# Where the ring of weights, the activations and the gated product begin in on-chip memory: three offsets modulo 2048 bytes in place of one

## The chip, the cores and the metric

The kernel runs on one core of a Trainium2 chip. The metric is the device time of one execution in microseconds. Addresses below are byte addresses within a partition of the on-chip memory (SBUF); each tensor occupies the same byte range in all 128 partitions.

## The reference

Two transformer blocks follow each other on 256 tokens of width 1024, all in float32. What matters here is that nearly all the work is products of activations with large weight matrices:

```
h = rmsnorm(x); proj = h @ w_in            # 1024 x 3072, then three mixers (two attentions, a short convolution)
x = x + group_rmsnorm(y) @ w_out           # 1024 x 1024
x = x + (silu(h @ w_gate) * (h @ w_up)) @ w_down      # 1024 x 2816, twice, and 2816 x 1024
# second block
h = rms_norm(x); proj = h @ w_in_2         # 1024 x 5888, spatial gating and a dilated attention
x = x + (gates[0] * (y_a @ w_branch_a) + gates[1] * (y_b @ w_branch_b)) @ w_out
up = h2 @ w_up; x = x + (gelu(conv(a)) * val) @ w_down; return rms_norm(x)
```

## The kernel before, in words

**Split precision.** Every float32 operand of a large product is split in two float32r tensors, a high part and the rest. A product is then three matmuls: high by high, high by low, low by high. The tensors that hold split activations are hx (the normalised input; hh and hl are its high and low half), yx (the mixer's output, later the second feed-forward's input; yh and yl) and G (the gated product of a feed-forward). Each has for each block of 128 features 256 high values and then 256 low ones, so 2048 bytes for a block.

**The ring.** The weights arrive as a stream of 113 units of 128 x 2048 values, numbered u = 0 to 112. Unit u lives in place u % 3 of a ring. SyncE starts its DMA into raw (line 456) when the unit three earlier has been split; ScalarE casts raw to whi (line 530, the high part) when TensorE is done with the unit three earlier; VectorE subtracts whi from raw into wlo (line 983, the low part); TensorE waits for that (`ready`) and uses the unit. raw, whi and wlo have three places each, 8192 bytes long, all of them allocated in a row, raw first.

**TensorE's instructions.** Each matmul loads its own stationary 128 x 128 tile (an LDWEIGHTS instruction) ahead of it, while the matmul before it streams. There are three kinds of unit:
- Pairs (`tiles`, lines 1606 and 1607): a 128 x 128 tile of whi is stationary and 512 columns stream (256 high, 256 low, adjacent in hx, yx or G); then the same tile of wlo with the 256 high columns alone. A unit has 16 pairs. The feed-forwards' gate and up products, the first down product and the second block's gate projections are of this kind: units 16 to 37 (hx), 38 to 48 (G), 61 to 71 (hx), 80 to 101 (yx).
- Narrow threes (`three`, lines 1599 to 1601): a tile of whi, again of whi and of wlo is stationary, and 256 columns of hx or yx stream. 48 matmuls a unit: units 6, 7, 9, 10, 11 and 76 to 79 (hx), 12 to 15 and 72 to 75 (yx). Unit 8 has the roles exchanged, 256 columns of whi or wlo streaming over tiles of hx.
- Wide threes (the same lines): hx or G is stationary and 512 columns of whi or wlo stream, 24 matmuls a unit: units 0 to 5 and 49 to 60 (hx), 102 to 112 (G).

**Addresses.** The allocator places tensors one after the other and starts each at a multiple of 32 bytes. A fixed region of 16384 bytes and four small constants of 32 bytes each come first, so raw begins at 16512, which is 128 modulo 2048. The nine ring places (8192 bytes each), sq (8192), hx (16384) and x follow. Therefore every place of raw, whi and wlo, and hx, begins at 128 modulo 2048. x has 8224 bytes, so yx after it begins at 160. G and gates share an address, behind a gap of LEAD float32 values, and begin at 128. All tiles that TensorE reads from these tensors lie at multiples of 512 bytes from the tensor's start.

Of the kernel before, what the change touches and what calls it, by code (L numbers as in the profile page):

```python
# [18 lines left out]
F32R = mybir.dt.float32r  # L19
# [5 lines left out]
P = 128  # L25
T = 256
TT = T // P
D = 1024
KT = D // P
# [3 lines left out]
UNIT = 16 * P  # L33
# [3 lines left out]
WARM_UP = 8  # L37
RING = 3

LEAD = 160  # L40

D_SB, D_CH, D_CV = 256, 512, 256
H_SB, H_CH = D_SB // HD, D_CH // HD
# [189 lines left out]
def build(nc, A, out):  # L233
    with ExitStack() as ctx:
        def sb(name, shape, dt=F32, scope=ctx):
            return scope.enter_context(nc.sbuf_tensor(name, shape, dt))
# [2 lines left out]
            return ctx.enter_context(nc.semaphore(name))  # L239

        raw = [sb(f"raw{s}", [P, UNIT]) for s in range(RING)]
        whi = [sb(f"whi{s}", [P, UNIT], F32R) for s in range(RING)]
        wlo = [sb(f"wlo{s}", [P, UNIT], F32R) for s in range(RING)]


        sq = sb("sq", [P, KT, T])
        hx = sb("hx", [P, KT, 2, T], F32R)

        x_gain = sb("x", [P, KT + KT * T])
        attn_gain, x = x_gain[:, 0:KT], x_gain[:, KT:KT + KT * T].rearrange("p (k t) -> p k t", k=KT)  # L250
        yx = sb("yx", [P, KT, 2, T], F32R)
        hh, hl = hx[:, :, 0, :], hx[:, :, 1, :]
        yh, yl = yx[:, :, 0, :], yx[:, :, 1, :]
        side = sb("side", [P, 2, T])
# [30 lines left out]
        sg = ExitStack()  # L285
        sb("before_G", [P, LEAD], scope=sg)
        G = sb("G", [P, FF_K, 2, T], F32R, scope=sg)
# [6 lines left out]
        s2 = ExitStack()  # L294
        sb("before_gates", [P, LEAD], scope=s2)
        gates = sb("gates", [P, 2, KT, T], scope=s2)
# [1940 lines left out]
```

## Time and profile before

| | |
|---|---|
| median of 3 runs | 692.86 us (692.68 to 693.03) |
| the profiled execution | 692.9 us, its span 691.2 us |
| TensorE matmul (PE) | busy 682.4 us, 99% of the span, 4118 instructions |
| weight load (PEld) | busy 601.3 us, 87% |
| VectorE (DVE) | busy 498.5 us, 72% |
| ScalarE (ACT) | busy 401.5 us, 58% |
| granted TensorE clock | 0.998 in the mean |

The span runs from the first to the last instruction; the rest of the time lies around it. The end of a matmul in the profile is modelled, and the modelled durations of adjacent matmuls overlap. So a matmul's cost is read from the distance between starts, not from its duration.

### The profile page before, as it was taken

How to read it: one execution, taken by the hardware profiler on the slowest of the kernel's cores; microseconds unless marked ns; L12 is line 12 of the kernel's file. 1: busy time of each engine (PE TensorE's matmuls, PEld its weight loads, DVE VectorE, ACT ScalarE, POOL GpSimd, SP SyncE). 2: the span in 40 equal slices, each digit the busy share in tenths (PEclk: the TensorE clock that was granted, in tenths of full speed). 3: DMA queues.
4: the chain of work that ended last, by engine and by line, in shares of the span. 5: the costliest groups of instructions: out<-in, count | busy, mean ns of one | idle time of the engine just before them, and what ended most of it. 6: DMA issues, size and time to landing. Idle time of an engine off the chain costs nothing.

```text
span 691.2 us, 10061 instructions
## 1 busy us (share of the span) xinstructions
PE 682.4 (99%) x4118; PEld 601.3 (87%) x4118; DVE 498.5 (72%) x689; ACT 401.5 (58%) x504; POOL 9.3 (1%) x25
## 2 busy tenths in 40 slices
PE   8999999999999999999999999999999999999996
PEld 7889999888888888888878888899988888888885
DVE  6866676979886766766565477687779988887453
ACT  7865865755555544455457565564557666664342
POOL 1000000003000000000000000000000000000000
PEclk9999999999999999999999999999999999999999
DMA  8863225655555555555435346444455555554511
GB/s 326 317 238 129 86 98 184 218 186 183 183 200 187 213 192 183 178 188 187 180 123 181 123 142 224 146 183 160 183 197 199 192 180 187 192 201 176 215 61 61
DMA packets 19773, 124.05 MB, mean 179 GB/s; under 512 B 2320, under 2 KB 3472, under 8 KB 5520
## 3 DMA queue, kind: packets, MB, share of 16 engines
q1 hardware_dynamic: 18432, 120.07, 48.7%
q10 hardware_dynamic: 1296, 3.35, 1.4%
q8 instruction: 32, 0.52, 0.3%
q14 instruction: 13, 0.11, 0.0%
HBM read 122.36 MB, written 1.05 MB: 179 GB/s over the span
## 4 chain that ended last, share of the span: by engine, by line
PE 90%; DVE 4%; ACT 3%; issue 1%; DMA 1%; DVEq 0%; ACTq 0%
PE psum L1606 34%; PE psum L1607 18%; PE psum L1599 10%; PE psum L1601 10%; PE psum L1600 10%; PE psum L1595 2%; DVE wlo L983 2%; ACT whi L530 2%; PE psum L1646 1%; PE psum L1649 1%; PE psum L2078 1%; PE psum L1652 1%; DMA x<-in_xT 1%; PE psum L2126 0%; DVE gates L1501 0%
## 5 line engine op out<-in xcount | busy, mean ns | idle before, releaser
L983 DVE TENSOR_TENSOR wlo<-raw,whi 128x2048 fp32r<-128x2048 f32 x110 | 251.7, 2290 | 76.4 <-ACT whi L530 76.4
L530 ACT CAST whi<-raw 128x2048 fp32r<-128x2048 f32 x110 | 209.6, 1908 | 42.8 <-PE psum L1601 37.7
L1606 PE MATMUL psum<-hx,whi 128*128 128x512 f32 x528 | 184.3, 395 | 0.0
L1607 PE MATMUL psum<-hx,wlo 128*128 128x256 f32 x528 | 146.9, 278 | 0.0
L1606 PE MATMUL psum<-yx,whi 128*128 128x512 f32 x352 | 123.2, 393 | 1.0 <-DVE yx L994 1.0
L1606 PEld LDWEIGHTS psum<-hx,whi 128*128 128x128 f32 x528 | 99.1, 188 | 23.3 <-issue 0.2
L1607 PEld LDWEIGHTS psum<-hx,wlo 128*128 128x128 f32 x528 | 99.4, 188 | 0.0
L1607 PE MATMUL psum<-yx,wlo 128*128 128x256 f32 x352 | 99.3, 282 | 0.0
L1606 PEld LDWEIGHTS psum<-yx,whi 128*128 128x128 f32 x352 | 66.1, 188 | 15.3 <-DVE yx L994 1.6
L1607 PEld LDWEIGHTS psum<-yx,wlo 128*128 128x128 f32 x352 | 66.7, 190 | 0.0
L1606 PE MATMUL psum<-G,whi 128*128 128x512 f32 x176 | 61.1, 394 | 0.0
L1599 PE MATMUL psum<-whi,hx 128*128 128x512 f32 (+1 forms) x144 | 55.9, 388 | 0.0
L1601 PE MATMUL psum<-whi,hx 128*128 128x512 f32 (+1 forms) x144 | 54.5, 378 | 0.0
L1600 PE MATMUL psum<-wlo,hx 128*128 128x512 f32 (+1 forms) x144 | 54.4, 378 | 0.0
L1607 PE MATMUL psum<-G,wlo 128*128 128x256 f32 x176 | 48.8, 277 | 0.0
L1599 PE MATMUL psum<-hx,whi 128*128 128x256 f32 x144 | 41.5, 288 | 0.1
L1601 PE MATMUL psum<-hx,wlo 128*128 128x256 f32 x144 | 40.8, 283 | 0.0
L1600 PE MATMUL psum<-hx,whi 128*128 128x256 f32 x144 | 40.8, 283 | 0.0
L1606 PEld LDWEIGHTS psum<-G,whi 128*128 128x128 f32 x176 | 33.0, 188 | 7.7
L812 ACT COPY us<-psum 128x512 f32<-128x512 f32 x22 | 12.9, 585 | 42.4 <-PE psum L1607 42.4
L805 ACT COPY side<-psum 128x512 f32<-128x512 f32 x22 | 12.8, 584 | 40.0 <-PE psum L1607 40.0
L1599 PE MATMUL psum<-yx,whi 128*128 128x256 f32 x128 | 36.0, 282 | 0.0
(271 smaller groups left out, 1107.7 us busy)
## 6 DMA issues: line engine op xcount, KB each, us to landing
raw<-in_stream SPq DMA_DIRECT2D x110, 1024.0 KB, 4.7
raw<-in_stream SPq DMA_DIRECT2D x8, 256.0 KB, 5.4
relb<-in_relb ACTq DMA_DIRECT2D x1, 1536.0 KB, 7.7
raw<-in_stream SPq DMA_DIRECT2D x2, 512.0 KB, 7.4
x<-in_xT SPq DMA_DIRECT2D x3, 256.0 KB, 5.6
out_t<-sq SPq DMA_DIRECT2D x4, 160.0 KB, 2.4
final_gain<-in_final_gain ACTq DMA_DIRECT2D x1, 512.0 KB, 3.7
bsp<-in_bsp ACTq DMA_DIRECT2D x1, 384.0 KB, 3.3
```

Of the source, the lines that this page charges most:

```text
L530: act.copy(whi[s][:], raw[s][:]).then_inc(unit_hi, 1)
L805: act.copy(side[:], psum[:, 0:2, T:2 * T]).then_inc(gate_side, 1)
L812: act.copy(us[:], psum[:, 2:4, T:2 * T]).then_inc(up_side, 1)
L983: dve.tensor_tensor(wlo[s][:], raw[s][:], whi[s][:], ALU.subtract).then_inc(unit_lo, 1)
L1595: return pe.transpose(out_, in_, ident[:])
L1599: pe.matmul(dst, stat[0], mov[0], start=first, stop=False, **kw)
L1600: pe.matmul(dst, stat[0], mov[1], start=False, stop=False, **kw)
L1601: return pe.matmul(dst, stat[1], mov[0], start=False, stop=last, **kw)
L1606: pe.matmul(bank[b][:], stat[0], mov, start=first, stop=False, skip_group_check=True)
L1607: return pe.matmul(bank[b][:, 0:T], stat[1], mov[:, 0, :], start=False, stop=last, skip_group_check=True)
L1646: pe.matmul(bank[6 + t][:], hh[:, k, c], whi[u][:, w], start=k == 0, stop=False)
L1649: pe.matmul(bank[6 + t][:], hh[:, k, c], wlo[u][:, w], start=False, stop=False)
```

## The change

hx moves in front of whi and wlo; whi and wlo of one place now stand together (whi0, wlo0, then whi1, wlo1, then whi2, wlo2); a gap of 32 bytes is put before the second and before the third place; yx moves between the second place and the second gap. LEAD falls from 160 to 144 values, which is 64 bytes less and takes up the two gaps. No instruction, wait or order changes.

```diff
-LEAD = 160
+LEAD = 144
...
         raw = [sb(f"raw{s}", [P, UNIT]) for s in range(RING)]
-        whi = [sb(f"whi{s}", [P, UNIT], F32R) for s in range(RING)]
-        wlo = [sb(f"wlo{s}", [P, UNIT], F32R) for s in range(RING)]
+        whi, wlo = [None] * RING, [None] * RING
+
+        def place(s):
+            whi[s] = sb(f"whi{s}", [P, UNIT], F32R)
+            wlo[s] = sb(f"wlo{s}", [P, UNIT], F32R)
+
+        hx = sb("hx", [P, KT, 2, T], F32R)
+        place(0)
+        sb("before_second", [P, 8])
+        place(1)
+        yx = sb("yx", [P, KT, 2, T], F32R)
+        sb("before_third", [P, 8])
+        place(2)
         sq = sb("sq", [P, KT, T])
-        hx = sb("hx", [P, KT, 2, T], F32R)
...
-        yx = sb("yx", [P, KT, 2, T], F32R)
```

Start modulo 2048, in bytes:

| tensor | before | after |
|---|---|---|
| raw, all three places | 128 | 128 |
| whi and wlo, place 0 / 1 / 2 | 128 / 128 / 128 | 128 / 160 / 192 |
| hx, G, gates | 128 | 128 |
| yx | 160 | 160 |
| sq, x | 128 | 192 |

What is allocated after x and before G (side, rb, cols, ident, ones and others), and the first block's mixer tensors, shift by 64 bytes. The second block's tensors behind LEAD keep their place.

## Rows read from the trace of the kernel before

**Rows 1.** The page: busy time and granted clock by fortieth.
```profile
PE 682.4 (99%) x4118; PEld 601.3 (87%) x4118; DVE 498.5 (72%) x689; ACT 401.5 (58%) x504; POOL 9.3 (1%) x25
...
PEclk9999999999999999999999999999999999999999
```

**Rows 2.** All waits of TensorE: who waited for whom, total us, times, longest.
```profile
PE psum L1947 <- POOL ones L474: 1.1, 1, 1.1
PE psum L1606 <- DVE yx L994: 1.0, 2, 0.5
PE psum L1646 <- ACT whi L535: 0.7, 1, 0.7
```

**Rows 3.** Groups of matmuls, kinds apart; names are moving,stationary.
```profile
L1606 PE MATMUL psum<-hx,whi 128*128 128x512 f32 x528 | 184.3, 395 | 0.0
L1606 PE MATMUL psum<-yx,whi 128*128 128x512 f32 x352 | 123.2, 393 | 1.0 <-DVE yx L994 1.0
L1606 PE MATMUL psum<-G,whi 128*128 128x512 f32 x176 | 61.1, 394 | 0.0
```

**Rows 4.** Line 1606 in four windows: hx, G, yx, then hx in the gates.
```profile
L1606 PE MATMUL psum<-hx,whi x305: 391/394/396, 138.7 to 244.1; 128*128 128x512 f32 x153
...
L1606 PE MATMUL psum<-G,whi x176: 391/394/396, 244.5 to 305.1; 128*128 128x512 f32 x176
...
L1606 PE MATMUL psum<-yx,whi x113: 389/390/391, 585.5 to 624.3; 128*128 128x512 f32 x113
...
L1606 PE MATMUL psum<-hx,whi x81: 394/398/404, 393.3 to 421.6; 128*128 128x512 f32 x81
```

**Rows 5.** Line 1599, narrow threes with hx, then with yx.
```profile
L1599 PE MATMUL psum<-hx,whi x49: 283/283/284, 481.1 to 498.4; 128*128 128x256 f32 x49
L1599 PEld LDWEIGHTS psum<-hx,whi x48: 191/192/193, 481.4 to 498.3; 128*128 128x128 f32 x48
...
L1599 PEld LDWEIGHTS psum<-yx,whi x64: 186/188/190, 452.9 to 474.9; 128*128 128x128 f32 x64
L1599 PE MATMUL psum<-yx,whi x64: 277/279/282, 453.0 to 475.0; 128*128 128x256 f32 x64
```

**Rows 6.** Line 1599, wide threes with G; line 1595, transposes.
```profile
L1599 PE MATMUL psum<-whi,G x64: 388/389/390, 635.5 to 678.4; 128*128 128x512 f32 x64
...
L1595 PE MATMUL psum<-ident,S x16: 271/273/273, 368.6 to 370.2; 128*128 128x128 f32 x16
```

**Rows 7.** Timeline: a matmul and the weight load for the next start together.
```profile
481.84 0.28 PE L1599 MATMUL psum<-hx,whi 128*128 128x256 f32 x1
481.84 0.19 PEld L1600 LDWEIGHTS psum<-hx,whi 128*128 128x128 f32 x1
481.96 0.28 PE L1600 MATMUL psum<-hx,whi 128*128 128x256 f32 x1
481.96 0.19 PEld L1601 LDWEIGHTS psum<-hx,wlo 128*128 128x128 f32 x1
```

**Rows 8.** The two splits of a unit from 60 to 680 us, and VectorE's wait.
```profile
L530 ACT CAST whi<-raw x103: 1885/1909/1932, 59.8 to 668.4; 128x2048 fp32r<-128x2048 f32 x103
  PE psum L1601: 36.6, 14
...
L983 DVE TENSOR_TENSOR wlo<-raw,whi x103: 2274/2292/2321, 61.7 to 670.4; 128x2048 fp32r<-128x2048 f32 x103
  ACT whi L530: 74.4, 69
```

**Rows 9.** Busy time by engine in one stretch.
```profile
139.10:244.40 105.30, 105.30 (x610) 92.04 (x609) 85.80 (x119) 56.01 (x58) 5.40 (x8) 1.00 0.54 190
```

## The prediction

> **What bounds the kernel now.** I read the page's busy times first: the matmul engine is busy for 682.4 of the span's 691.2 us, at full granted clock in every fortieth [rows 1]. Next its waits: three entries, 2.8 us in all [rows 2]. So the weights are always there in time, and the time is the sum of the distances between matmul starts. The third view is one line's first and last start with its count, which gives that distance. Pairs with hx streaming: 305 starts from 138.7 to 244.1 us, so 105.4/304 = 346.7 ns a pair. With G: 60.6/175 = 346.3. With yx: 38.8/112 = 346.4 [rows 4]. Narrow threes with hx: 48 threes in 17.3 us, 120.1 ns a matmul. With yx: 63 threes in 22.0 us, 116.4 ns [rows 5]. Wide threes: 63 in 42.9 us, 227.0 ns [rows 6].
>
> The reader is to see two things. First, 256 columns more cost 227.0 - 120.1 = 107 ns, so a matmul of 256 columns has about 13 ns that are not streaming, and one of 512 too; a pair has 346.7 - 3 x 107 = 26, again 13 each. These 13 ns are the only thing that a changed address can move. Second, the narrow threes with yx are 3.7 ns shorter than those with hx, with the same shapes and weights. What differs is the address: yx begins at 160 modulo 2048, hx and the weights at 128. Each matmul starts together with the weight load for the next [rows 7], and with hx that load too is recorded longer (192 against 188 ns) [rows 5]. So where the streamed operand begins relative to the loaded one does matter, in that one kind. In the pairs the same 32 bytes make no difference: 346.4 with yx, 346.7 and 346.3 with hx and G, and the readings are good to 1 ns.
>
> **The change part by part.** No instruction is added, removed or moved. I write the offset as streamed minus weights. Today it is 0 with hx and G and +32 with yx. After: with hx and G it is 0, -32, -64 in places 0, 1, 2; with yx +32, 0, -32. Where the weights stream (wide threes) it is 0, +32, +64.
>
> Pairs. There are 1056 [rows 3]. Units by place (u % 3): units 16 to 37 give 7, 8, 7 in places 0, 1, 2; units 38 to 48 give 4, 3, 4; units 61 to 71 give 3, 4, 4; units 80 to 101 (yx) give 7, 7, 8. Places 0, and place 1 of yx, have offsets that the trace shows, and they cost the same (346.3 to 346.7): nothing there. New are -32 in 8+3+4+8 = 23 units, 368 pairs, and -64 in 7+4+4 = 15 units, 240 pairs: 608 pairs. Bounds: the dearest row of a pair is the gates', 28.3/80 = 353.8 ns, 7.1 more [rows 4]; from below, a 128-column load and matmul need 1.6/15 = 107 ns in the transposes [rows 6], which allows a 256-column matmul 13 less and a pair 26 less. Far apart, so I take the nearest rows, which are pairs at 0 and at +32: no change. Ends kept: -15.8 us (608 x 26 ns) and +4.3 us (608 x 7.1 ns).
>
> Narrow threes. hx in place 1 (units 7, 10, 76, 79) and place 2 (11, 77), and unit 8, where the weights stream at +64: 7 x 48 = 336 matmuls leave the offset 0, which costs 120.1. They can fall to 116.4 or stay; I take half of it: -336 x 1.85 ns = -0.62 us, ends -1.24 and 0. yx in place 1 (13, 73): 96 matmuls come to the offset 0, so 3.7 ns each: +0.36. yx in place 2 (14, 74): 96 at -32, half: +0.18, ends 0 and +0.36. The sum is -0.08 us.
>
> Wide threes. Place 1 (units 1, 4, 49, 52, 55, 58, 103, 106, 109, and half of 112) and place 2 (2, 5, 50, 53, 56, 59, 104, 107, 110): 228 + 216 = 444 matmuls at +32 and +64. They are 512-column matmuls as half of the pairs' are, and pairs did not care for +32: nothing. Ends: -3.7 ns each as in the threes, -1.6 us; +3.5 each (half of the gates' 7.1), +1.6.
>
> A rule of the Trainium skill bears on this. The page "TensorE: Matmul & The Clock Gate", in "Step-by-step: what each phase is for", says that TensorE reads SBUF through two independent ports, so that loading the next weights takes nothing from the running matmul. The trace disagrees in one kind, 120.1 against 116.4 ns; by that rule every term here would be nothing and the time that of before.
>
> The engines beside it. ScalarE's casts take 1885 to 1932 ns and VectorE's subtractions 2274 to 2321, while TensorE reads another place all the time [rows 8]. So narrow a spread over 103 units leaves nothing that staggered places could save them. If they changed anyway, VectorE waits 74.4 us for the casts and ScalarE 36.6 for TensorE [rows 8], and that cover holds: a cast 5% longer is 0.1 us against those waits. In the other direction, pairs kept to 391 to 396 ns [rows 4] while VectorE was busy for 85.8 and ScalarE for 56.0 of 105.3 us [rows 9], so their accesses don't slow TensorE. The shift by 64 bytes of x, sq and the first mixer's tensors touches short operations and float32 matmuls; priced at nothing, as all these stay multiples of 32 from where they were; if ten of the short ones on the path grew by 10 ns it would be 0.1 us.
>
> Sum: 0 - 0.08 + 0 = -0.1 us on the profiled execution's 692.9 (span 691.2 and 1.7 around it), so 692.8. The median of the runs is 692.86, the same to 0.1.
>
> **The rivals.**
> (B) The 13 ns shrink wherever the offset isn't 0, as in the threes. For it: 120.1 against 116.4 ns. Against it: the pairs with yx, at +32, have kept their 26. In full, 1216 matmuls of the 608 pairs and 444 wide ones lose 3.7 ns each, -4.5 and -1.6, and the narrow ones -1.24 + 0.36: -7.0 us, 685.9. If only one of the two negative offsets does it, about half: 689.4.
> (C) The other side, slower. The gates show that the same instructions at the same addresses can run in a dearer rhythm: 353.8 ns a pair for more than 28 us, from the small attention matmuls on until other small ones follow, and in nothing else different from the 346.7 [rows 4]. If the load begins 32 or 64 bytes ahead of the streamed operand, it may meet it in the same place of the memory shortly after the start, and the matmuls lock into that rhythm. Place: the pairs at a negative offset. Price: 608 x 7.1 = +4.3, with the yx threes' +0.72 in full: 697.9. With -32 alone (368 pairs, +2.6, and +0.7): 696.2. With -64 alone (240 pairs, +1.7, and +0.4): 695.0. It decides as soon as some 200 pairs are in it, for that is 1.4 us. For it: the rhythm exists. Against it: it appears only in 6 of 66 units, and yx's offset never brought it.
> (D) The placement doesn't do what it says, or is of no consequence, the threes included: 692.9. In the numbers this is my forecast.
>
> **How the numbers follow.** A measurement of this kernel tells about 0.2%, 1.4 us, from no change. My forecast with (D): 0.46. B in full or part: 0.29. C: 0.25. All of the forecast's own spread (-1.24 to +0.72) is within 0.2%: 691.6 to 693.6. B lies below 691.5 and C above 694.3. So faster 0.29, same 0.46, slower 0.25. The range takes in C whole but for its last part and the nearer half of B: 688.0 to 697.2.
>
> **What would show it.** The starts of line 1606 by unit: 346.7 ns a pair in all three places would bear me out; 340 or so in places 1 and 2 of units 16 to 60 shows B; 353 there shows C. Line 1599 in units 77 and 78, next to each other in places 2 and 0, gives the threes' effect within one stage; units 72 to 75 give yx at +32, 0 and -32. L530 and L983 should keep 1909 and 2292 ns. I am wrong if the pairs move by more than 2 ns in either new offset, or if the gates' dear stretch (units 61 to 66) ends or spreads: its end alone is 96 x 7.1 = -0.7 us. A change in the other kernel-wide quantities (granted clock, waits of TensorE over 3 us) would mean that I read the wrong resource.

## The result and the profile after

The changed kernel takes 699.24 us (699.17 to 699.81, four runs) against 692.94: a ratio of 1.0095 with a 95% interval of 1.0083 to 1.0107; the medians lie 6.3 us apart. The prediction was 692.8 with a range up to 697.2. The profiled execution took 699.8 us, its span 698.1, which is 6.9 more than before.

The page after. Work and clock are as they were, and the matmul engine's busy time has grown by the whole difference [rows 1]:
```profile
PE 689.3 (99%) x4118; PEld 602.6 (86%) x4118; DVE 498.6 (71%) x689; ACT 401.1 (57%) x504; POOL 9.4 (1%) x25
...
PEclk9999999999999999999999999999999999999999
```

Line numbers are higher by 10. All waits of TensorE after; 3.0 us where it was 2.8 [rows 2]:
```profile
PE psum L1616 <- DVE yx L1004: 1.2, 3, 0.5
PE psum L1957 <- POOL ones L484: 1.1, 1, 1.1
PE psum L1656 <- ACT whi L545: 0.7, 1, 0.7
```

Line 1616, pairs in the first feed-forward and the down product (they answer to rows 4):
```profile
L1616 PE MATMUL psum<-hx,whi x305: 388/398/403, 139.3 to 246.6; 128*128 128x512 f32 x153
...
L1616 PE MATMUL psum<-G,whi x176: 388/398/403, 247.0 to 308.8; 128*128 128x512 f32 x176
```
A pair costs 107.3/304 = 353.0 ns with hx (346.7 before) and 61.8/175 = 353.1 with G (346.3). The mean over the three places leaves no room for a cheap place. The timeline shows them one by one; these are the first matmuls of units 33, 34, 35 and 36, in places 0, 1, 2, 0, sixteen pairs apart:
```profile
218.71 0.40 PE L1616 MATMUL psum<-hx,whi 128*128 128x512 f32 x1
...
224.37 0.39 PE L1616 MATMUL psum<-hx,whi 128*128 128x512 f32 x1
...
230.03 0.40 PE L1616 MATMUL psum<-hx,whi 128*128 128x512 f32 x1
...
235.66 0.40 PE L1616 MATMUL psum<-hx,whi 128*128 128x512 f32 x1
```
5.66, 5.66 and 5.63 us: 353.8 ns in place 0 (offset 0, as before the change), 353.8 in place 1 (-32), 351.9 in place 2 (-64). **Place 0 is as dear as the others, although its own offset did not change.** (These distances run from unit to unit and take in the step between two units.)

The wide threes (first matmuls of units 103 to 106, places 1, 2, 0, 1; 24 matmuls apart) and the narrow ones with hx (units 77, 78, 79 and what follows; 48 apart):
```profile
636.15 0.40 PE L1609 MATMUL psum<-whi,G 128*128 128x512 f32 x1
...
641.76 0.40 PE L1609 MATMUL psum<-whi,G 128*128 128x512 f32 x1
...
647.26 0.39 PE L1609 MATMUL psum<-whi,G 128*128 128x512 f32 x1
...
652.73 0.40 PE L1609 MATMUL psum<-whi,G 128*128 128x512 f32 x1
```
```profile
486.14 0.28 PE L1609 MATMUL psum<-hx,whi 128*128 128x256 f32 x1
...
491.59 0.28 PE L1609 MATMUL psum<-hx,whi 128*128 128x256 f32 x1
...
497.35 0.28 PE L1609 MATMUL psum<-hx,whi 128*128 128x256 f32 x1
...
503.03 0.40 PE L1616 MATMUL psum<-yx,whi 128*128 128x512 f32 x1
```
Wide: 233.8 ns at +32, 229.2 at +64, 227.9 at 0, where all were 227.0 [rows 6]. Narrow: 113.5 ns at -64, 120.0 at 0, 118.3 at -32, where all were 120.1 [rows 5].

Where the time went, from the starts of the same matmuls in both traces: for each unit the mean distance of undisturbed starts times the number of matmuls, difference after minus before, in us.

| kind | place 0 | place 1 | place 2 | sum |
|---|---|---|---|---|
| pairs with hx, G (units 16 to 71) | +1.36 | +1.26 | +1.18 | +3.8 |
| pairs with yx | +0.07 | +0.63 | +0.63 | +1.3 |
| wide threes | +0.19 | +1.42 | +0.46 | +2.1 |
| narrow threes | +0.04 | +0.02 | -0.55 | -0.5 |

Together +6.7 of the span's +6.9 us. A single entry depends by 0.1 us or so on which starts are counted as undisturbed.

### The profile page after: what moved, and what is told of

Its sections match the earlier page's. It is cut to its first block, busy times and chain, and to the rows that moved or that the text cites. A ratio compares the mean times of both kernels' runs of the same rounds, so it can differ in the third digit from the quotient of the medians.

```text
span 698.1 us, 10061 instructions
## 1 busy us (share of the span) xinstructions
PE 689.3 (99%) x4118; PEld 602.6 (86%) x4118; DVE 498.6 (71%) x689; ACT 401.1 (57%) x504; POOL 9.4 (1%) x25
## 4 chain that ended last, share of the span: by engine, by line
PE 91%; DVE 4%; ACT 3%; issue 1%; DMA 1%; DVEq 0%; ACTq 0%
PE psum L1616 35%; PE psum L1617 18%; PE psum L1609 10%; PE psum L1611 10%; PE psum L1610 10%; PE psum L1605 2%; DVE wlo L993 2%; ACT whi L540 2%; PE psum L1656 1%; PE psum L1659 1%; PE psum L2088 1%; PE psum L1662 1%; DMA x<-in_xT 1%; PE psum L2136 0%; DVE gates L1511 0%
## 5 line engine op out<-in xcount | busy, mean ns | idle before, releaser
L1616 PE MATMUL psum<-hx,whi 128*128 128x512 f32 x528 | 186.9, 398 | 0.0
L1616 PE MATMUL psum<-yx,whi 128*128 128x512 f32 x352 | 124.7, 397 | 1.2 <-DVE yx L1004 1.2
L1616 PEld LDWEIGHTS psum<-yx,whi 128*128 128x128 f32 x352 | 66.1, 188 | 17.3 <-DVE yx L1004 2.1
```

The source lines that it names most:

```text
L1616: pe.matmul(bank[b][:], stat[0], mov, start=first, stop=False, skip_group_check=True)
```

## The experiments

**Theories.** H: the cost of a matmul follows from the offset (streamed minus weights; the expectation of the first run calls this part R), and pairs have besides that two rhythms, about 346.7 and 353.3 ns a pair, one of which is handed on from unit to unit. Rivals: the order and neighbourhood of the tensors or the other engines' writes cost the time (O, E); each unit pays for its own offset alone (L); only the change of offset from unit to unit is dear (M); the rhythm belongs to the addresses and nothing else changes it (N).

In all layouts below LEAD is set so that G and gates stand as said. First four layouts, run together.

**The order alone.** hx first, whi and wlo of a place together, all places at 128:
```diff
         hx = sb("hx", [P, KT, 2, T], F32R)
         place(0)
-        sb("before_second", [P, 8])
         place(1)
-        yx = sb("yx", [P, KT, 2, T], F32R)
-        sb("before_third", [P, 8])
         place(2)
+        sb("gap0", [P, 8])
+        yx = sb("yx", [P, KT, 2, T], F32R)
```


> The changed order of allocation (hx first, whi and wlo of a place together) with all three places at 128 modulo 2048, hx and G at 128, yx at 160: the offsets of before, and the rest of the memory shifted by 32 bytes. Theory R (relative offset, streamed minus weights, is all that counts): 692.9 us, pairs at 346.7 ns in all places, narrow threes 120 with hx and 116.7 with yx. Rival O (the order, or the neighbourhood of raw, whi and wlo, or the shift of the small tensors costs the time): 699 us. Between them if both have a part.

Measured: 693.31 us, ratio 1.0005 (0.9996 to 1.0014). Line 1615, the same stretch as in rows 4, 105.4/304 = 346.7 ns:
```profile
L1615 PE MATMUL psum<-hx,whi x305: 391/391/391, 138.9 to 244.3; 128*128 128x512 f32 x153
```
O is out: the order, with the rest of the memory shifted by 32 bytes, costs nothing that can be measured.

**Place 1 alone at 160**, places 0 and 2 at 128:
```diff
         place(0)
-        sb("before_second", [P, 8])
+        place(2)
+        sb("gap0", [P, 8])
         place(1)
         yx = sb("yx", [P, KT, 2, T], F32R)
-        sb("before_third", [P, 8])
-        place(2)
```


> Place 1 alone at 160; places 0 and 2 at 128; hx, G 128, yx 160. Theory H (rhythm handed on: TensorE's pairs have two rhythms, 346.7 and about 353.5 ns, a unit at offset -32 throws them into the dear one and a later unit at offset 0 stays in it): places 0 and 2 are dear as well, 353.7 ns with hx and G, some 38 units by 16 pairs by 6.8 ns = +4.1 us, place 1 with yx +0.7, wide threes of place 1 (228 by 6.8 ns) +1.6, narrow ones about 0: 699.3 us. Rival L (each unit pays for its own offset alone): only place 1 is dear, 13 units by 16 by 6.7 = +1.4, +0.7, +1.6: 696.6 us, with 346.7 ns in places 0 and 2.

Measured: 698.48 us, ratio 1.0082 (1.0067 to 1.0097). Units 33 to 36 again (places 0, 1, 2, 0):
```profile
218.35 0.40 PE L1615 MATMUL psum<-hx,whi 128*128 128x512 f32 x1
...
224.00 0.39 PE L1615 MATMUL psum<-hx,whi 128*128 128x512 f32 x1
...
229.65 0.39 PE L1615 MATMUL psum<-hx,whi 128*128 128x512 f32 x1
...
235.29 0.40 PE L1615 MATMUL psum<-hx,whi 128*128 128x512 f32 x1
```
5.65, 5.65 and 5.64 us, 353 ns in every place. Place 0 follows place 2, both at offset 0 as before the change, and is dear all the same. So L (696.6) is out; the time is 0.8 us below H's 699.3. Where the dear rhythm begins can be seen too. These are the first matmuls of units 16 and 17 and the last pair of unit 17, fifteen pairs on:
```profile
121.99 0.39 PE L1615 MATMUL psum<-hx,whi 128*128 128x512 f32 x1
...
127.53 0.40 PE L1615 MATMUL psum<-hx,whi 128*128 128x512 f32 x1
...
132.84 0.40 PE L1615 MATMUL psum<-hx,whi 128*128 128x512 f32 x1
```
Unit 16, in place 1 at -32, took 346 ns a pair, and unit 17, in place 2 at offset 0, 354. No other matmul stands between the two, and with all places at 128 unit 17 ran at 346.7. So it was not a dear unit at -32 that handed its rhythm on, as H had it: here the rhythm switched where the offset went from -32 to 0, and the later units kept it.

**All places 32 bytes on, and all 64 bytes on**, constant offsets:
```diff
         hx = sb("hx", [P, KT, 2, T], F32R)
+        sb("gap0", [P, 8])
         place(0)
-        sb("before_second", [P, 8])
         place(1)
+        place(2)
         yx = sb("yx", [P, KT, 2, T], F32R)
-        sb("before_third", [P, 8])
-        place(2)
```
(This is the first of the two, with yx behind the places at 160; in the second, yx at 160 and another 32 bytes stand between hx and the places at 192.)

> All three places at 160, yx 160, hx and G 128: the offset is -32 everywhere with hx and G, 0 with yx, +32 where weights stream. Theory H (the offset -32 is dear in itself): pairs with hx and G 353.4 ns (+4.1 us), pairs with yx 346.7, wide threes 233.5 (700 by 6.8 ns, +4.8), narrow hx 118.3 (432 by -1.7, -0.7), narrow yx 120 (384 by 3.3, +1.3): 702.4 us. Rival M (mixing: only the change of offset from unit to unit breaks the rhythm; a constant offset runs cheaply): pairs 346.7 and wide threes 226.7 everywhere, 693.5 us.

> All three places at 192, yx 160, hx and G 128: -64 with hx and G, -32 with yx, +64 where weights stream. Theory H (each offset has its own price, which a constant one keeps): pairs hx and G 352.4 ns (38 units by 16 by 5.7, +3.5), pairs yx 353.4 (352 by 6.7, +2.4), wide threes 229.4 (700 by 2.7, +1.9), narrow hx 115.7 or 113.7 (432 by -4.3 to -6.3, -1.9 to -2.7), narrow yx 118.2 (384 by 1.5, +0.6): 699.0 us. Rival M (mixing alone is dear): 346.7 and 226.7, the narrow ones as said: 691.5 us, faster than both kernels.

Measured: 701.92 us, ratio 1.0133 (1.0118 to 1.0148), and 698.63 us, ratio 1.0076 (1.0059 to 1.0093). At -32 everywhere, pairs and wide threes:
```profile
L1615 PE MATMUL psum<-hx,whi x301: 392/402/402, 139.9 to 245.9; 128*128 128x512 f32 x151
...
L1608 PE MATMUL psum<-whi,G x62: 393/395/397, 637.0 to 679.7; 128*128 128x512 f32 x62
```
106.0/300 = 353.3 and 42.7/183 = 233.3 ns. At -64 everywhere, pairs and narrow threes:
```profile
L1616 PE MATMUL psum<-hx,whi x303: 397/397/398, 138.8 to 245.5; 128*128 128x512 f32 x152
...
L1609 PE MATMUL psum<-hx,whi x51: 276/276/276, 483.9 to 500.9; 128*128 128x256 f32 x51
```
106.7/302 = 353.3 and 17.0/150 = 113.3 ns. M is out: a constant offset doesn't run cheaply, and both times came within 0.5 us of H's. But a pair's offset doesn't fix its price. In the kernel with all places 64 bytes on, yx is at -32 throughout the second feed-forward, and yet units 88 to 91 ran in the cheap rhythm. The second pair of unit 88 and the first of unit 89, fifteen pairs apart, 5.20/15 = 346.7 ns:
```profile
550.59 0.39 PE L1616 MATMUL psum<-yx,whi 128*128 128x512 f32 x1
...
555.79 0.39 PE L1616 MATMUL psum<-yx,whi 128*128 128x512 f32 x1
```
Units 87 and 92 took 353. The rhythm changed at the four transposes ahead of unit 88 and at those behind unit 91, not at those between units 89 and 90. And in the first of these two kernels yx is at a constant offset of 0, and its pairs change their price without any change of address. The first and last pair of units 84, 87 and 89, fifteen pairs apart:
```profile
529.41 0.39 PE L1615 MATMUL psum<-yx,whi 128*128 128x512 f32 x1
...
534.61 0.39 PE L1615 MATMUL psum<-yx,whi 128*128 128x512 f32 x1
...
546.59 0.40 PE L1615 MATMUL psum<-yx,whi 128*128 128x512 f32 x1
...
551.89 0.40 PE L1615 MATMUL psum<-yx,whi 128*128 128x512 f32 x1
...
558.23 0.39 PE L1615 MATMUL psum<-yx,whi 128*128 128x512 f32 x1
```
346.7 ns in unit 84, 353.3 in unit 87 (and 346.7 again in unit 89, by its starts to 563.43). From unit 84 on the switch comes each time where four transposes stand between two units (after units 85, 87, 89 and 91). There was one more: units 80 and 81 were dear, and the product of the row statistics behind unit 81 was followed by the cheap rhythm.

**One interruption, and two, in the kernel before**, whose addresses stay as they are:
```diff
                 for i in range(FF_STEPS):
...
+                    if (blk, i) == (0, 2):          # the other kernel: blk == 0 and i in (2, 4)
+                        for _ in range(4):
+                            transpose(bank[5][:, 0:P], ident[:])
```


> The kernel before, all addresses as they were, with four transposes of the identity once, ahead of unit 20 in the first feed-forward. Theory H (at offset 0 pairs have two rhythms, kept until something interrupts them, and an interruption by transposes toggles them, as it did four times in the second feed-forward with all places at 160): units 20 to 48 run at 353.3 ns a pair, 29 x 16 x 6.6 ns = +3.1 us, with +0.5 for the transposes: 696.5 us. Rival N (the rhythm belongs to the addresses): all stay at 346.7, +0.5 alone: 693.4 us.

> As the one before, with four more transposes ahead of unit 24. Theory H (toggle): units 20 to 23 at 353.3 ns, from 24 on at 346.7 again, 4 x 16 x 6.6 ns = +0.4 us and +1.0 for the transposes: 694.3 us. Rival S (transposes set the dear rhythm rather than toggle it): 353.3 from 20 on to 48, 697.0 us. Rival N: 693.9 us.

Measured: 696.17 us, ratio 1.0051 (1.0036 to 1.0067), and 696.34 us, ratio 1.0057 (1.0043 to 1.0071). With one interruption, line 1606 ahead of it and behind it:
```profile
L1606 PE MATMUL psum<-hx,whi x16: 392/394/396, 138.6 to 143.8; 128*128 128x512 f32 x16
...
L1606 PE MATMUL psum<-hx,whi x288: 394/399/476, 144.9 to 246.4; 128*128 128x512 f32 x144
```
```profile
144.53 0.60 PE L1595 MATMUL psum<-ident 128*128 128x128 f32 x4
144.89 0.48 PE L1606 MATMUL psum<-hx,whi 128*128 128x512 f32 x1
```
5.2/15 = 347 ns a pair ahead, 101.5/287 = 353.7 behind, up to the end of the down product and over 460 pairs. Four matmuls that hold TensorE for half a microsecond cost 3.6 (the kernel before measured 692.57 beside this run). N is out: this is the kernel before, with its addresses. The second interruption did not switch back (line 1606 behind it, 78.9/223 = 353.8 ns):
```profile
L1606 PE MATMUL psum<-hx,whi x224: 394/398/478, 167.7 to 246.6; 128*128 128x512 f32 x112
```
So at offset 0 an interruption does not simply toggle; my "toggle" (694.3) was wrong. Rival S, by which transposes set the dear rhythm, was right on the rhythm here (its time, 697.0, was 0.7 too high), but not in the kernel with all places 32 bytes on, where they also ended it.

**Can an interruption save the changed kernel's place 0?** The same four transposes ahead of each unit of place 0 in its first feed-forward.

> The changed kernel with four extra transposes of the identity (into a free PSUM bank) ahead of each unit of place 0 in the first feed-forward, 7 units at offset 0. Theory H (two rhythms, the state is TensorE's own and is reset or toggled where other matmuls interrupt the pairs): those 7 units drop from 353.7 to 346.7 ns a pair, places 1 and 2 stay at 353.4 and 352.4; the transposes with their entry cost about 0.65 us each time, so 7 x (0.65 - 0.11) = +3.8 us, 703.0 us in all. Rival E (other engines: place 0 is dear because ScalarE and VectorE write at other alignments in the neighbouring places meanwhile): the 7 units stay at 353.7 ns, 703.8 us.

Measured: 702.22 us, ratio 1.0133 (1.0118 to 1.0149). Unit 18 from its second to its last pair, then unit 21:
```profile
134.33 0.40 PE L1616 MATMUL psum<-hx,whi 128*128 128x512 f32 x1
...
139.19 0.39 PE L1616 MATMUL psum<-hx,whi 128*128 128x512 f32 x1
...
151.61 0.39 PE L1616 MATMUL psum<-hx,whi 128*128 128x512 f32 x1
...
156.56 0.40 PE L1616 MATMUL psum<-hx,whi 128*128 128x512 f32 x1
```
4.86/14 = 347.1 ns in unit 18, 4.95/14 = 353.6 in unit 21, and 352.7 to 353.5 in the other five. The time doesn't tell the theories apart (703.0 and 703.8 were expected), the units do: H expected seven cheap ones and got one; E expected none. That one, with the same neighbours and the same other engines' work, speaks against E. What sets unit 18 apart is that a product of the row statistics stands ahead of the transposes there; whether that is the reason was not tried.

**Offsets in the other direction.** hx, G and yx at +32; then hx +64, G and yx +96; then hx and G +128, yx +256; the ring uniform at 128.
```diff
-        hx = sb("hx", [P, KT, 2, T], F32R)
         place(0)
...
         place(2)
+        sb("gap0", [P, 8])          # 16 and 32 values in the other two
+        hx = sb("hx", [P, KT, 2, T], F32R)
+        yx = sb("yx", [P, KT, 2, T], F32R)     # behind 8 and 32 more values in the other two
```


> The ring as before (all at 128), hx, G and yx all at 160: the offset is +32 in every pair and narrow three, -32 where weights stream. Theory H: +32 has only the cheap rhythm in pairs (yx before), so the six gate units drop from 353.2 to 346.7 (-0.6 us) and the narrow threes with hx from 120 to 116.7 (432 matmuls, -1.4 us). The wide threes (720) are not known at -32. If they stay at 226.7 ns: 690.9 us, faster than both kernels; rival W (in wide threes any offset but 0 is dear, 233 as at +32): 695.8 us.

> The ring at 128, hx at +64, G and yx at +96. Theory H with a range of good offsets (the streamed operand ahead of the loaded one is good in pairs): pairs 346.7 or less, narrow threes 116.7 or less, about 691 us if the wide threes keep 226.7, 696 if they take 233. Rival P (the effect repeats every 64 bytes, so +64 is like 0 and +96 like +32): narrow hx 120, narrow yx 116.7, pairs 346.7, gates 353, 693 us. No theory has a firm number for these offsets; the distances by unit are what is asked.

> The ring at 128, hx and G at +128, yx at +256. Rival P in its wider form (the effect repeats every 128 bytes): everything as at offset 0, narrow threes 120 ns with hx and with yx, pairs 346.7 with the gates 353, yx narrow +1.3 us: 694.2 us. Otherwise new values by unit, which bound how far an offset reaches: if the streamed operand well ahead is free of the load's reads until they part, narrow threes come down towards 113 and the time to 688-690 us.

Measured: 695.67 us, ratio 1.0035 (1.0023 to 1.0048); 698.99, ratio 1.0089 (1.0071 to 1.0108); 699.97, ratio 1.0103 (1.0085 to 1.0122). With all at +32 the gates' dear stretch is gone, as expected, and the narrow threes with hx came down to 116.7 to 117.8 ns; but rival W was right for the wide ones:
```profile
L1608 PE MATMUL psum<-whi,G x58: 395/396/396, 639.6 to 679.5; 128*128 128x512 f32 x58
```
39.9/171 = 233.3 ns. Of the third kernel, the pairs in the first feed-forward:
```profile
L1616 PE MATMUL psum<-hx,whi x301: 387/396/398, 138.9 to 244.3; 128*128 128x512 f32 x151
```
105.4/300 = 351.3 ns at +128. Its yx, at +256, behaved as at 0: 120.0 ns in the narrow threes and a rhythm that switched between 346.7 and 353.3 at the same places. In the second kernel the pairs with hx, at +64, took 348.9 ns (353.3 in the gates) and those with G and yx, at +96, 349.9; its wide threes took 233 to 234. The two wider shifts (two runs each) had no firm forecast: the time was 3.0 us above the nearer of H's two for the second kernel, and 6 us above what the rivals with a period of 64 and of 128 bytes said. So neither of these is the period.

**Places apart by 256 bytes** (128, 384, 384; yx at 416):
```diff
         place(0)
-        sb("before_second", [P, 8])
+        sb("gap0", [P, 64])
         place(1)
+        place(2)
+        sb("gap1", [P, 8])
         yx = sb("yx", [P, KT, 2, T], F32R)
-        sb("before_third", [P, 8])
-        place(2)
```


> Places at 128, 384, 384 modulo 2048, hx and G at 128, yx at 416: no two engines' tensors stand as before, and the offset changes from place to place by 256 bytes. Theory H with a period of 256 bytes: as offset 0 and +32 everywhere, pairs 346.7 ns in all places, 692.9 us. Rival E (absolute places and their neighbours count, or the period is longer than 256): pairs at 350 to 353.5 ns in places 1 and 2 or in all, wide threes above 227, 696 to 699 us.

Measured: 693.19 us, ratio 1.0006 (0.9996 to 1.0015). Line 1616, 104.4/301 = 346.8 ns:
```profile
L1616 PE MATMUL psum<-hx,whi x302: 391/391/391, 138.9 to 243.3; 128*128 128x512 f32 x151
```
Staggering the ring is harmless as such, and what counts is the offset modulo 256 bytes: the layouts at +32, +64, +96 and +128 differ from offset 0, so that no smaller step will do. E is not settled by this layout alone, because raw, whi and wlo keep their relative starts modulo 256 in it. What speaks against E is the layout with all at +32, whose ring stands as before while its wide threes took 233.3 ns, and the single interruption, which moved no address.

**Two versions meant to beat both.** A uniform ring, hx and G at its offset, yx at +32; the narrow threes of the output and branch products (units 12 to 15 and 72 to 79) read hx and yx through a second view, 64 bytes ahead of the weights modulo 256. In the second version the branch products (72 to 75) read yx at +32 again:
```diff
+        hx_room = sb("hx", [P, 16 + KT * 2 * T], F32R)
...
+        yx_room = sb("yx", [P, 24 + KT * 2 * T], F32R)
+        hx, hx_n, yx, yx_n = view(hx_room, 16), view(hx_room, 0), view(yx_room, 24), view(yx_room, 0)
...
-                        ins = three(bank[b][:, 0:T], (whi[s][:, w], wlo[s][:, w]), (hh[:, k, :], hl[:, k, :]),
+                        ins = three(bank[b][:, 0:T], (whi[s][:, w], wlo[s][:, w]), (hh_n[:, k, :], hl_n[:, k, :]),
```


> A version meant to beat both: the ring in one place (all at 192), hx and G at the same offset 0, yx at +32 for its pairs as before; but hx and yx get 64 and 96 bytes more room, and the narrow threes of w_out (both blocks) and of the two branches read them through a second view that begins 64 bytes before the weights modulo 256. The price list found so far says 113.4 ns a matmul at -64, against 120 (hx, 192 matmuls: -1.3 us) and 116.7 (yx, 384: -1.3 us), all else as before: 690.3 us. Rival V (the offset repeats with more than 256 bytes, so yx's view at -64 modulo 256 alone has another price, or the pairs fall into the dear rhythm after the changed entries): 691.6 us in the first case, up to +2.3 us for one feed-forward in the dear rhythm in the second, 693 to 695 us.

> As the version with two views, but the branch products (units 72 to 75) read yx at +32 again, where they ran at 116.7 ns against 117.8 at -64. Left are w_out of the first block (192 matmuls, 116.7 to about 114.5 by the last run's units: -0.4 us) and of the second (192, 120 to 113.3: -1.3 us): 691.0 us. Rival: the gain of 1.7 us is eaten by the entries of the stages (the last run's trace gained 1.6 us in these units and its span only 0.5): 692.2 us, no difference to be measured.

Measured: 692.22 us, ratio 0.9993 (0.9984 to 1.0002), and 692.56, ratio 0.9998 (0.9990 to 1.0007): no difference to be measured. The price list held in part. In the second version's trace units 77 to 79 take 16.3 us where they took 17.3, 113.3 ns a matmul. But in the first version the branch products, at the same -64 modulo 256, did not come down to that price:
```profile
L1607 PE MATMUL psum<-yx,whi x63: 280/282/282, 452.9 to 474.8; 128*128 128x256 f32 x63
```
21.9/186 = 117.7 ns, more than the 116.6 that they cost at +32. So narrow threes too have more than one price at one offset. Units 12 to 15, through the same view, ran at 113 to 116; what makes the difference was not tried. What was gained in units 77 to 79 was lost again: the next stage starts earlier and waits longer. All of TensorE's waits between 497 and 512 us, in the second version:
```profile
PE psum L1614 <- DVE yx L1002: 1.8, 3, 0.8
```
That was 1.0 us [rows 2]. The version reached unit 80 at 497.38 us against 498.76, and unit 82 at 511.36 against 511.70: of 1.4 us, 0.3 were left, and 0.8 of the 1.0 lost are this longer wait for the normalised input, which comes from VectorE.

## Why the prediction was wrong

**The bound** was right: matmul distances are the time; TensorE's waits stayed at 3 us and the work and clock were the same.

**"Places 0, and place 1 of yx, have offsets that the trace shows, and they cost the same [...]: nothing there"** is the step that failed. It took a pair's cost for a function of the unit's own offset. Place 0 costs 353.8 ns a pair and +1.36 us, place 1 of yx 353.3 in six of its seven units and +0.63. My own rows had the warning: the gates ran at 353.8 ns at the very same addresses [rows 4]. I used that row as a price and overlooked what it says of causes: that the rhythm depends on what came before. The kernel with place 1 alone moved, and the one with a single interruption, show that. What in TensorE or the memory keeps such a rhythm stays open.

**The pairs at -32 and -64, "no change"**: 353.3 and 351.9 to 353.3 ns. These 608 pairs measured +3.1 us, nearer to the upper end that I had kept, +4.3, than to nothing. That end was too high: four of its 38 units (61, 62, 64, 65) stand in the gates and were dear before, and units 61 and 80, at -32, ran at 346.6 and 347.4 ns after. The nearest row (+32) was the wrong neighbour, since the sign matters: +32 kept 346.7 ns in all 22 units of a feed-forward, -32 did so in some units only.

**The wide threes, "nothing"**, were mis-sized: 233.8 and 229.2 ns, +1.9 us in places 1 and 2 where I had kept +1.6 as an end. "Pairs did not care for +32" does not carry over to them.

**The narrow threes** were right in sign and small: -0.5 us measured, -0.08 said. My ends add up to -0.88 and +0.72; the -1.24 in my text leaves out the +0.36 of place 1 of yx. Returning to offset 0 cost yx 2.9 ns a matmul (119.6), -64 gave hx 6.6, more than I had allowed.

**The engines beside it, the shift by 64 bytes**: right. The casts took 1886 to 1934 ns and the subtractions 2277 to 2319, as before [rows 8], and the order alone, with a shift by 32 bytes, cost 0.3 us, within its interval of nothing. The shift by 64 has no run of its own; the 0.2 us that the table leaves of the 6.9 bound it.

**Rival C** named the mechanism, the gates' dear rhythm, but placed it only in pairs at a negative offset. With place 0, place 1 of yx and the wide threes it comes to the measured +6.3; in its full form it had +5.0.

## What to carry to other kernels

When a matmul loads its stationary tile from the same memory from which the other operand streams, try the two operands' relative start in steps of 32 bytes, for each kind of matmul separately, and count it modulo 256 bytes: here 128, 160, 192 for the places of a ring cost 0.95%, 160 for all of them 1.33%, while one step of 256 bytes cost nothing. The same offset in all places is thus no remedy; of the uniform layouts only offset 0 (with yx at +32) was as fast as the kernel before. Read distances between starts by unit; a stretch that is 2% slower at unchanged addresses is a sign of a rhythm that is handed on, and then one unit's price cannot be read from that unit alone, nor the price of an offset from one stage. A gain on the busiest engine ahead of a normalisation may come back as a wait.

## What the runs showed of the hardware that I had not expected

- Pairs have two rhythms, 346.7 and 353.3 ns, at offset 0 and at -32; one interruption of half a microsecond switched 460 pairs. At +32 only the cheap one was seen, at -64 only the dear one. Which one an interruption leaves was not settled: four transposes switched both ways in the kernel with all places 32 bytes on, and only once in the kernel before with two interruptions.
- The price by offset: narrow threes 120 ns (0), 116.7 to 117.8 (+32), 118.3 (-32), 113.3 or 117.8 (-64); wide threes 226.7 in a uniform layout (0) and 229 to 234 at every other offset tried, modulo 256.
- The Trainium skill, in "TensorE: Matmul & The Clock Gate", "Step-by-step: what each phase is for", calls the two read ports independent. The runs disagree in so far as the relative address of two reads changes a matmul's distance by 2 to 7 ns. That the two reads meet in one part of the memory is an argument from this and from the repetition by 256 bytes; no run shows it directly.
